# The mixing factor of differential attention: from one VectorE instruction to two GpSimd products

## The reference, cut to what matters

```python
lam = exp(sum(lam_q1 * lam_k1)) - exp(sum(lam_q2 * lam_k2)) + lambda_init
s = einsum('mbhqd,mbhkd->mbhqk', q_blk, k) * scale
p = softmax(s, axis=-1)
a = p[0] - lam * p[1]
o = einsum('bhqk,bhkv->bhqv', a, v)
```

## Time and profile before

| | |
|---|---|
| median of 3 runs | 983.8 us (982.41 to 983.94) |
| span of the profiled execution, first to last instruction | 980.4 us; its own time is not listed apart, the median of the runs is 3.4 us above the span |
| TensorE busy | 967.6 us, 99% |
| VectorE busy | 853.5 us, 87% |
| ScalarE busy | 457.9 us, 47% |
| GpSimd busy | 377.8 us, 39% |
| granted TensorE clock | 1.000 of full speed |
| `mixc` instructions | 32, the first at 86.6 us, the last at 252.4 us |

### The profile page before, as it was taken

How to read it: one execution, slowest core, us unless ns; L and a number is a source line. 1 busy time by engine, 2 the same in 40 slices (tenths; PEclk the granted TensorE clock), 3 DMA queues, 4 the chain that set the end, 5 groups by cost and what they waited for, 6 DMA issues and landing times.

```text
span 980.4 us, 12869 instructions
## 1 busy us (share of the span) xinstructions
PE 967.6 (99%) x4684; PEld 796.9 (81%) x4684; DVE 853.5 (87%) x1157; ACT 457.9 (47%) x703; POOL 377.8 (39%) x333
## 2 busy tenths in 40 slices
PE   9999999989999999999999999999999999999998
PEld 7887877767887878888888888988888888888887
DVE  6696999999777999999989888779898988989883
ACT  6445654666556253552534534475345253452520
POOL 6841453335463828467534000551340413405000
PEclk9999999999999999999999999999999999999999
DMA  7333220200251432423334250304342332422202
GB/s 264 87 107 102 72 65 1 65 22 22 66 171 44 135 123 87 129 87 101 114 87 128 65 172 23 129 1 129 87 129 87 108 107 87 129 86 86 87 1 86
DMA packets 50966, 90.12 MB, mean 92 GB/s; under 512 B 8268, under 2 KB 9560, under 8 KB 50904
## 3 DMA queue, kind: packets, MB, share of 16 engines
q1 hardware_dynamic: 45456, 89.14, 29.0%
q10 hardware_dynamic: 5448, 0.17, 0.3%
HBM read 87.20 MB, written 2.10 MB: 91 GB/s over the span
## 4 chain that ended last, share of the span: by engine, by line
PE 63%; DVE 5%; POOL 2%; issue 1%; ACT 1%; POOLq 0%; DVEq 0%; ACTq 0%
PE bank L1711 32%; PE pair L1711 30%; POOL s_nsum L766 1%; DVE s_acc L1476 1%; DVE s_lbB_lo L1225 1%; DVE s_lt_lo L1225 1%; DVE s_w_lo L1198 1%; DVE s_acc L1545 0%; DVE s_s_raw L1461 0%; PE bank L2070 0%; DVE s_u_raw L1443 0%; PE pair L2058 0%; DVE s_hT_lo L1425 0%; POOL s_lt L792 0%; ACT s_hT_hi L1037 0%
## 5 line engine op out<-in xcount | busy, mean ns | idle before, releaser
L792 POOL TENSOR_TENSOR s_lt<-s_lbB,s_lbB 128x1024 f32<-128x1024 f32 x14 | 34.5, 2466 | 263.4 <-PE pair L1711 163.9
L1198 DVE TENSOR_TENSOR s_w_lo<-s_raw,s_w_hi 128x1024 fp32r<-128x1024 f32 x72 | 127.5, 1791 | 3.7 <-ACT s_w_hi L871 3.7
L1225 DVE TENSOR_TENSOR s_lbB_lo<-s_lbB,s_b_hi 128x1024 fp32r<-128x1024 f32 x64 | 119.0, 1883 | 0.0
L893 ACT ACTIVATE s_b_hi<-s_lbB 128x1024 fp32r<-128x1024 f32 x64 | 67.2, 1053 | 77.0 <-POOL s_lbB L792 32.9
L1711 PE MATMUL bank<-s_hT_hi,s_w_hi 128*128 128x512 f32 x256 | 100.2, 392 | 0.0
L1711 PE MATMUL pair<-s_hT_hi,s_w_hi 128*128 128x512 f32 x256 | 100.1, 391 | 0.0
L1711 PE MATMUL bank<-s_hT_hi,s_w_lo 128*128 128x512 f32 x256 | 99.6, 389 | 0.0
L1711 PE MATMUL bank<-s_hT_lo,s_w_hi 128*128 128x512 f32 x256 | 99.6, 389 | 0.0
L1711 PE MATMUL pair<-s_hT_hi,s_w_lo 128*128 128x512 f32 x256 | 99.6, 389 | 0.0
L1711 PE MATMUL pair<-s_hT_lo,s_w_hi 128*128 128x512 f32 x256 | 99.6, 389 | 0.0
L1057 ACT ACTIVATE s_u_raw<-s_u_raw 128x512 f32<-128x512 f32 x64 | 40.4, 632 | 111.6 <-DVE s_u_raw L1443 111.6
(11 more groups left out here) (268 smaller groups left out, 2699.3 us busy)
## 6 DMA issues: line engine op xcount, KB each, us to landing
s_raw<-in_mlp_w SPq DMA_DIRECT2D x64, 512.0 KB, 3.7
s_lbB<-in_mlp_w SPq DMA_DIRECT2D x64, 512.0 KB, 3.3
s_raw<-in_attn_w_qkv SPq DMA_DIRECT2D x24, 512.0 KB, 4.1
s_raw<-in_attn_w_o SPq DMA_DIRECT2D x8, 512.0 KB, 3.3
s_x_nat<-in_x SPq DMA_DIRECT2D x4, 512.0 KB, 6.4
out<-s_acc SPq DMA_DIRECT2D x7, 256.0 KB, 2.0
s_raw<-in_pool_w SPq DMA_DIRECT2D x4, 256.0 KB, 2.7
out<-s_acc SPq DMA_DIRECT2D x2, 128.0 KB, 1.8
```

Of the source, the lines that this page charges most:

```text
L792: g.tensor_tensor(w2_raw[n][:], w2_raw[one][:], w2_raw[two][:], ALU.subtract).then_inc(t_done, 1)
L893: a.activation(b_hi[home][:], w2_raw[n][:], ACT.Copy).then_inc(w2_hi_done, 1)
L1198: v.tensor_tensor(w_lo[slot][:, cols], raw[k][:], f32(w_hi[slot][:, cols]), ALU.subtract)\
L1225: v.tensor_tensor(w2_lo[n][:], w2_raw[n][:], f32(b_hi[home][:]), ALU.subtract).then_inc(w2_lo_done, 1)
```

## The change

GpSimd gets `mix_factor`; VectorE's is taken out. GpSimd first multiplies the first row sum by `neg_lam` into a new tile `l0n` and waits for the end of that, then waits for VectorE's reciprocal (`mix_rooted`) and multiplies the two into `mixc`, counting `mix_known`, for which `combine` waits as before. It waits for `exp_done` (the row sum) and for `a_done` of two steps ago (the buffers). The call for step i - 1 is the first thing in GpSimd's step i. `mix_root`, `maxima` and `combine` stay on VectorE in their order.

```diff
--- before.py
+++ after.py
@@ -333,6 +333,7 @@
         lsum = sb("lsum", [P, STEPS, 2])
         rl1 = sb("rl1", [P, 2])
         mixc = sb("mixc", [P, 2, 1])
+        l0n = sb("l0n", [P, 2, 1])
         o_ss = sb("o_ss", [P, NT])
         o_sq = sb("o_sq", [P, NT])
         o_v = sb("o_v", [P, NT])
@@ -391,6 +392,7 @@
         max_done = sem("max_done")
         exp_done = sem("exp_done")
         mix_rooted = sem("mix_rooted")
+        l0_scaled = sem("l0_scaled")
         mix_known = sem("mix_known")
         a_done = sem("a_done")
         turned = sem("turned")
@@ -720,7 +722,19 @@
                 qk_square(n)
                 qk_root(n - 1)
             qk_root(2 * NT - 1)
+            def mix_factor(i):
+
+                pool.wait_ge(exp_done, 2 * i + 1)
+                if i >= 2:
+                    pool.wait_ge(a_done, i - 1)
+                link(g.tensor_tensor(l0n[:, i % 2, :], lsum[:, i, 0:1], neg_lam[:, 0:1], ALU.mult))
+                pool.wait_ge(mix_rooted, i + 1)
+                g.tensor_tensor(mixc[:, i % 2, :], l0n[:, i % 2, :], rl1[:, i % 2:i % 2 + 1], ALU.mult)\
+                    .then_inc(mix_known, 1)
+
             for i in range(LAST + 1):
+                if 1 <= i <= STEPS:
+                    mix_factor(i - 1)
                 if i >= 7 and (i - 7) % NT == 0:
 
                     h = (i - 7) // NT
@@ -1362,12 +1376,6 @@
                 dve.wait_ge(exp_done, 2 * i + 2)
                 v.reciprocal(rl1[:, i % 2:i % 2 + 1], lsum[:, i, 1:2]).then_inc(mix_rooted, 1)
 
-            def mix_factor(i):
-
-                dve.wait_ge(mix_rooted, i + 1)
-                v.scalar_tensor_tensor(mixc[:, i % 2, :], lsum[:, i, 0:1], neg_lam[:, 0:1], rl1[:, i % 2:i % 2 + 1],
-                                       ALU.mult, ALU.mult).then_inc(mix_known, 1)
-
             def combine(i):
 
                 q = i % 2
@@ -1387,8 +1395,6 @@
                     mix_root(i - 1)
                 if i < STEPS:
                     maxima(i)
-                if 1 <= i <= STEPS:
-                    mix_factor(i - 1)
                 if 2 <= i < STEPS + 2:
                     turn_lo("map", i - 2)
                 if 1 <= i <= STEPS:
```

## The result

The changed kernel takes 984.62 us, the median of 20 runs (983.4 to 986.22), against 982.85 us for the kernel before in the same measurement (20 runs, 981.64 to 983.94). The ratio is 1.0018, with a 95% interval of 1.0012 to 1.0025, so it is slower by about 1.8 us. I had forecast slower by 3.5, and had said that I would count less than 0.2% as no change; the time lies just inside that line, a result to which I had given 0.27, and the interval leaves no doubt that it is slower. A second measurement of the changed kernel, beside the experiments, gave 984.04 against 982.39, ratio 1.0021 (1.0012 to 1.0030).

What follows compares the result with a forecast made beforehand. TensorE alone bounds the attention's first half; in the second it and VectorE pace each other. Terms -1.0 + 2.5 + 0.2 + 0.4 + 1.4 + 0 + 0 = +3.5 us gave 987.3 us, range 982.3 to 991.5.

Steps and rivals of the forecast that it cites:

- Step 8, +2.5: Attention step 8: GpSimd's power and `oc` wait behind `mixc` for VectorE's late reciprocal, delaying TensorE; +2.1 to +3.9 us.
- Step 12, +0.2: Attention step 12: `oc` done at 158.7 to 159.0 against a turn at 159.42; 0 to 0.7 us lost.
- step 16, +0.4: Attention step 16: `oc` done at 181.4 against a turn at 181.34; +0.1 to +1.1 us.
- Steps 20 to 32, +1.4: Head turns of steps 20, 24, 28, 32: `oc`, already waited for, comes later; +1.4 us, bounds 0.5 and 2.6.
- Relief, -1.0: VectorE without `mixc`: half of 2.1 us of queue time in the attention's second half gained; bounds 0 and -4.9 us.
- moved work, 0: GpSimd's `x_kept` and `x_added` sums start behind the reciprocal: -1.0 in step 21, two losses of 0.5; bounds -1.5, +2.
- Half of the VectorE queue time as a gain: Second half of the attention: 16 `mixc` at 0.13 us give 2.1 us, half of it taken as won.
- GpSimd late for the factor, 0: Steps 2 to 12: `mixc` late behind GpSimd's roots and squares, but TensorE should not see it; bounds 0 and +1 us.
- rival (b): GpSimd's queue bounds the early steps, late factors of steps 6, 10, 11 reaching TensorE; +8 us, 991.8, chance 0.09.
- The product, 0.20: Each new 128x1 product on GpSimd takes 0.20 us, bounds 0.09 and 0.48.
- Rival (c): The products themselves hold up VectorE on SBUF, 4.8 us in the second half on top; 992 us, chance 0.05.
- Rival (a): VectorE's relief wins through TensorE's idle time from 190 to 256 us, so not slower; up to 982.0 us, chance 0.26.

Runs made afterwards that it cites:

- e1: Changed kernel with GpSimd's two factor products behind the head's power and scaling in every step, instead of ahead; 980.64 against 982.24 us, ratio 0.9985.
- e3: Kernel before, `mixc` staying on VectorE, with GpSimd waiting for the step's reciprocal at the start of each step; 983.02 against 982.24 us, ratio 1.0006.
- e2: Changed kernel with the products behind the head's power and scaling in step 8 alone; 982.36 against 982.24 us, ratio 1.0002.
- e10: Changed kernel with the products behind the head's power and scaling in steps 8 and 12 only; 981.65 against 982.39 us, ratio 0.9992.
- e4: Kernel before with the factor left out, `combine` taking the reciprocal instead (result incomplete), no product or wait added; 980.35 against 982.24 us, ratio 0.9982.
- e11: Kernel before with the factor left out and, from step 20 on, GpSimd's sums held to the reciprocal; 980.72 against 982.39 us, ratio 0.9982.
- e6: Changed kernel with VectorE's reciprocal moved earlier, directly behind the previous step's `combine`; 980.54 against 983.51 us, ratio 0.9973.
- e5: Kernel before with GpSimd waiting for the step's reciprocal ahead of its sums only, from step 20 on; 981.13 against 983.51 us, ratio 0.9979.
- e8: Kernel before with GpSimd waiting for the reciprocal ahead of its sums in step 21 alone; 982.24 against 983.51 us, ratio 0.9989.
- e7: Changed kernel with two more unused 128x1 products, each with its `link`, behind the two of each step; 991.24 against 983.51 us, ratio 1.0078.

## Why the prediction was right or wrong

The direction was right, and so was the mechanism of the loss; the size was twice too large, because the gain at step 21 was under-priced and small losses were added up that did not come. No rival took place. By the steps of the forecast, with the table above:

- **Step 8, +2.5.** Measured +2.31. The chain came as worked out: `w_lo` in 2.73 us (forecast 2.7), the reciprocal at 132.97 less the 1.08 of the later start, 131.9 (forecast 131.75), then `mixc`, power and `oc` unstretched. Shown by e1 and e3. The forecast took the granted clock as 1.00 throughout; the executions at 0.998 add about 0.2 us to the median.
- **Step 12, +0.2; step 16, +0.4.** Measured 0 and 0. I had laid each against TensorE's time of before, and TensorE came 2.3 us later. For step 12 this is what hid it: e2 takes the delay of step 8 away, and +0.93 appears. A delay upstream hides those downstream, and I added them up all the same. For step 16 it is not: in e10 nothing is late upstream, and step 16 still costs 0. There `oc` was ready at 180.73, just ahead of the weight load at 180.79, so the +0.4 was too much by itself.
- **Steps 20 to 32, +1.4.** The place was right, the size too large. The waits before these turns went from 2.9 to 3.6 us (6.1 - 2.5), and the steps of the turns lost 0.16, 0.12, 0.37 and 0, together 0.65. e10 against e1, 0.07% or 0.7 us in the runs, is of the same size.
- **Relief, -1.0, and moved work, 0.** These are the terms that failed. Step 21 alone gave -1.84, and step 25 another -0.19. It is the moved work that gave them, the term that I had put at 0: e3 holds the sums with no relief at all and has the same -1.82 and -0.18. I had seen the step 21 collision and priced it -1.0, by the 1.08 us of the stretch of `w_lo`. TensorE idled there 1.07 us for the low half of `oT` and another 0.46 for the exponentials, and both went. Then I had set two losses of 0.5 against it, steps 18 and 25 to 30. Step 18 shows none; e3, with `mixc` still on VectorE, loses 0.47 in steps 18 and 19, so there the relief seems to pay for it. Of the other there is +0.24 in step 27: the two sums of step 26 (228.25 to 230.79 us) now meet `combine`, which takes 1.66 us, and TensorE waits 0.28 us for the exponentials that come after it.

```profile
229.67 1.66 DVE L1383 SCALAR_TENSOR_TENSOR s_p<-s_p,s_mixc 128x512 f32<-128x512 f32 x1
```

  With -2.03 where I had -1.0 and 0, the sum is 2.31 + 0.65 - 2.03 + 0.24 + 0.21 (behind step 29) = +1.4, which is the trace. The lower end of the range was also added up wrongly: it takes -2.1 for the relief, though I had given -4.9 as its bound.
- **Half of the VectorE queue time as a gain.** e4 measures the relief by itself at 1.9 us, but two thirds of it (1.25) lie in step 21, in the same wait that held sums remove; e11 shows that the second cure brings nothing more there. The relief was not a rate over the stretch, but mostly one wait.
- **GpSimd late for the factor, 0.** Right. It happened, in step 6, where `mixc` stands behind the square; GpSimd and VectorE of the changed kernel:

```profile
118.82 1.04 POOL L704 TENSOR_TENSOR s_qsq<-s_qs 128x512 f32<-128x512 f32 x1
120.09 0.19 POOL L732 TENSOR_TENSOR s_mixc<-s_l0n,s_rl 128x1 f32<-128x1 f32 x1
```
```profile
120.31 0.75 DVE L1383 SCALAR_TENSOR_TENSOR s_p<-s_p,s_mixc 128x512 f32<-128x512 f32 x1 [0.89 <-POOL s_mixc L732]
```

  TensorE did not see it: up to 190 us its only idle time is the 2.07 us of step 8. That also decides rival (b), which needed these waits to reach TensorE.
- **The product, 0.20.** Both products by line (ns min/median/max, first and last start):

```profile
L730 POOL TENSOR_TENSOR s_l0n<-s_lsum,s_neg_lam x32: 185/190/692, 81.9 to 252.9; 128x1 f32<-128x1 f32 x32
L732 POOL TENSOR_TENSOR s_mixc<-s_l0n,s_rl x32: 189/190/192, 82.9 to 254.7; 128x1 f32<-128x1 f32 x32
```

  Each takes 0.19 us, against 0.21 for the one operation on VectorE. The first product does get stretched, to 0.64 at 203.89: it ends at 204.53, when `combine` (203.23, 1.25) has ended; but it lies ahead of its wait. `combine` is held in step 8 (1.26 at 134.82) by `oc`, not by a product. Rival (c) wanted 4.8 us from the products in the second half. e11 has no products and VectorE's relief as well; from step 16 on the changed kernel is 1.2 us behind it, all of that in the later heads' steps and step 27, and in every other step, 21 among them, the two agree within 0.05 us. So (c) is not borne out.

  The Trainium skill, "GPSIMD Engine Reference", section 3.1, has its ratio of 1.96 from an addition of 2048 elements in each partition; my estimate of 0.41 us from it does not hold for one element. The Trainium skill, "SBUF — State Buffer", section "SBUF: two separate sides", says that of a VectorE operation with two SBUF inputs and a GpSimd operation that reads SBUF the one that starts first holds their shared ports to its end. The stretched product, which ends at 204.53 just behind `combine`, agrees.
- **Rival (a)** had the right force and asked too much of it: TensorE's idle time from 190 to 256 fell by 0.7 us, not by the 3.1 that were needed. Without the queue order it is what happens: e1 and e6 are faster than before.

**What stays open.** e3 and e5 hold the sums and keep `mixc` on VectorE, and both win 0.9 us behind the last map's turn, after a loss of 0.2 to 0.5 just ahead of it; the changed kernel and e11, which hold the sums too, do not. The traces show where: at the first values behind that turn. In e3 the last `combine` (255.50) starts before the sums (255.66) and takes 0.75 us; in the kernel before it starts after them (254.68 against 254.44) and takes 1.59, in the changed kernel likewise (256.97 against 256.90, 1.76). `o_keep`, behind it in VectorE's queue, then ends 0.94 us after the turn in e3, but 1.96 before and 2.14 in the changed kernel, where TensorE waits for it, 0.58 and 0.76 us. No run moves this collision by itself, so its price is read off and not shown. Nor is it known where the clock fell in the executions at 0.998.

## What to carry to other kernels

Ahead of putting a wait in an in-order queue, list what is already runnable behind it and who needs it next: two products of 0.19 us cost 0.17 us, but a power and a scaling held behind them cost 2.3 us in one step, and putting them first, or making the awaited value earlier, turned a loss of 0.2% into a gain of 0.15 to 0.27%. Gains and losses are read per step and not added blindly: an upstream delay hides the ones behind it, and two cures of one wait count once. A wait may also help, by keeping deferrable work of one engine off the moment in which another engine needs the same memory: one such wait in one step was worth 0.11% (e8).

## What the runs showed of the hardware

- A wait of TensorE of about 2 us was followed by a fall of its clock in some executions and not in others. In e7 the granted clock fell from 1.00 to 0.50 twice, for 3.4 us each, after 3.00 and after 1.94 us of idle time; in step 8 that added some 1.4 us to a wait of 3.4. In the profiled executions of the changed kernel and of e3 it stayed at 1.00 after 2.07 and 1.87 us. But 11 of the 31 executions of the changed kernel and 3 of the 11 of e3 have a mean of 0.998, which is what one such stretch would give (an estimate: 1.7 us lost in 983), and none of the 86 of the kernels without a wait in step 8 (e1, e2, e4, e5, e6, e8, e10, e11), whose longest idle time in the attention is 1.1 us in the profiles; of the kernel before it is 1 of 85.
- A 128x1 product on GpSimd takes 0.19 us when nothing holds it up, no more than the 0.21 of the 128x1 operation that it replaces on VectorE. One that must wait for its own predecessor on the queue follows it after 0.27 us (two in e7 take 0.53 of the queue).
- The power over 128x4 elements takes 1.01 us, as long as a 128x512 product (1.04); it is half of what stood behind the wait.
